# Delta stage's end of a two-layer trunk kernel: output tile 0 read back in the last round, last stores awaited one stage later, last sample states in their own buffer

## What is computed

```
cs = silu(c);  per layer i: mod = cs @ w_ada[i] + b_ada[i]  -> shift, scale, gate for mixer and for MoE
h = x * (1 + scale_m) + shift_m
y = retention(h)            for layer 0   (4 heads, dk 256, dv 512)
y = gated_delta_net(h)      for layer 1   (16 value heads of 128 x 128, causal conv of width 4)
x = layer_norm(ALPHA * x + (1 + gate_m) * y)
h = x * (1 + scale_f) + shift_f
y = moe(h)                  16 experts in 4 groups, top 2, one shared router
x = layer_norm(ALPHA * x + (1 + gate_f) * y)
outputs: y_prompt, y_sample, and the new recurrent states of both mixers and of the convolution
```

## Time and profile before

| | us |
|---|---|
| three timed runs | 2217.83 median, 2215.38 to 2229.18 |
| the profiled execution | 2212.75 |
| its span, first to last instruction | 2210.9 |
| PE busy in the span | 1863.6 (84%) |
| granted TensorE clock, mean over the span | 0.908 of full speed |
| delta's first projection to the first product of mixer_end for layer 1 | 1024.4 to 1806.7 |
| DMA traffic | 397.20 MB, mean 180 GB/s |
| of it in the two queues named "instruction" | 2.28 MB |

### The profile page before, as it was taken

The page is one execution under the profiler, slowest core; times in us unless marked ns, Lnnn a source line. Parts: engine busy times, 40 slices in busy tenths (PEclk is TensorE's granted clock), DMA queues, the critical chain, the costliest instruction groups (busy, mean ns, idle before and its releaser), DMA issues. The chain is left out here.

```text
span 2210.9 us, 35700 instructions
## 1 busy us (share of the span) xinstructions
PE 1863.6 (84%) x15037; PEld 971.6 (44%) x15037; DVE 795.4 (36%) x1646; ACT 378.8 (17%) x835; POOL 355.6 (16%) x456
## 2 busy tenths in 40 slices
PE   5999999999899859956989989988987769949970
PEld 3443443433334432324566656755754634433320
DVE  0123323223322330015665465555535323240008
ACT  1010000100000011114332242232232100001111
POOL 0010110101102200022521122032031002120114
PEclk8999999999989979977989989989998779959985
DMA  9364638457170199978321033034035574078964
GB/s 341 123 226 174 255 121 295 164 177 255 68 248 38 43 379 398 398 276 270 129 93 46 15 116 110 12 106 121 8 108 159 177 217 137 27 270 298 403 241 147
DMA packets 234652, 397.20 MB, mean 180 GB/s; under 512 B 17597, under 2 KB 90949, under 8 KB 234438
## 3 DMA queue, kind: packets, MB, share of 16 engines
q1 hardware_dynamic: 228542, 373.43, 48.1%
q0 software_dynamic: 5952, 21.50, 2.6%
HBM read 301.38 MB, written 93.51 MB: 179 GB/s over the span
## 5 line engine op out<-in xcount | busy, mean ns | idle before, releaser
L562 PE MATMUL bank<-ring,hT 128*128 128x512 f32 x768 | 346.5, 602 | 3.3 <-PEq L277 2.2
L562 PEld LDWEIGHTS bank<-ring,hT 128*128 128x128 f32 x768 | 142.8, 191 | 189.2 <-issue 186.5
L1194 PE MATMUL bank<-hT,ring 128*128 128x272 f32 x768 | 220.3, 422 | 0.0
L2344 PE MATMUL bank<-expert_w,exp_xT 128*32 128x512 f32 x1152 | 177.9, 625 | 14.4 <-DMA expert_w<-in_moe_w_gu_dram 10.4
L3020 PE MATMUL bank<-ring,oT 128*128 128x512 f32 x384 | 174.7, 617 | 13.3 <-DMA oT<-oT_spill 12.7
L1194 PEld LDWEIGHTS bank<-hT,ring 128*128 128x128 f32 x768 | 142.8, 199 | 35.0 <-issue 9.5
L1188 PE MATMUL bank<-ring,hT 128*128 128x512 f32 x256 | 125.0, 617 | 0.0
L3020 PEld LDWEIGHTS bank<-ring,oT 128*128 128x128 f32 x384 | 75.4, 198 | 108.0 <-issue 94.9
L2344 PEld LDWEIGHTS bank<-expert_w,exp_xT 128*32 128x32 f32 x1152 | 47.5, 115 | 125.6 <-issue 120.4
L2368 PE MATMUL bank<-expert_w,exp_aT 128*32 128x512 f32 x576 | 88.7, 606 | 10.6 <-DMA expert_w<-in_moe_w_down_dram 9.2
L1864 DVE SCALAR_TENSOR_TENSOR dn_y<-dn_pre,dn_conv,dn_y 128x568 f32<-128x568 f32 x96 | 89.3, 930 | 3.4
(11 more groups left out here) (478 smaller groups left out, 2559.8 us busy)
## 6 DMA issues: line engine op xcount, KB each, us to landing
ring<-in_w_ada_dram SPq DMA_DIRECT2D x24, 2048.0 KB, 9.2
expert_w<-in_moe_w_gu_dram SPq DMA_DIRECT2D x24, 2048.0 KB, 15.8
expert_outputs<-ret_zeros SPq DMA_DIRECT2D x15, 2048.0 KB, 10.4
expert_w<-in_moe_w_down_dram SPq DMA_DIRECT2D x24, 1024.0 KB, 16.3
ring<-in_ret_w_in_dram SPq DMA_DIRECT2D x8, 2048.0 KB, 13.9
ret_Ss<-in_state_ret_dram SPq DMA_DIRECT2D x32, 512.0 KB, 5.5
out_dram<-ret_Ss SPq DMA_DIRECT2D x32, 512.0 KB, 3.9
oT<-in_moe_w_gu_dram SPq DMA_DIRECT2D x8, 2048.0 KB, 21.0
```

What stands on the lines that cost most here:

```text
L562: last = pe.matmul(ps[u % 2][:, :], core.hT[:, k, tok(t)], core.ring[:, w % RING, k, :], start=(k == 0), stop=(k == KD - 1))
L1194: mm = pe.matmul(ps[U % 2][:, 0:HALF], core.ring[:, w % RING, k, c * P:(c + 1) * P], core.hT[:, k, half * HALF:(half + 1) * HALF], start=( ...
L2344: last = pe.matmul(ps[v][G * j:G * (j + 1), :], xT[:, v, k, G * j:G * (j + 1)], wgu[of[j] % SLOTS][:, k, :], start=(k == 0), stop=(k == KD ...
```

## The change

- `state_in`: state 7 (the last, `n == 2 * G - 1`) goes to `SLAST`, laid over the first half of `qr`, whose last user is round 2. It is loaded without a wait in SP's step C3 of the last chunk of round 2, behind the store of `S`. The loads of states 1 to 6 are as they were. PE's S1 waits for both of the last two loads from state 6 on.
- `va` and `qr` become pairs of buffers; the first of `va` is `core.reuse`, which outlives the stage. In C5 of x = 13 SP waits for store 12 and reads tile 0 of oT_spill (1 MB) into it (`first_tile`, semaphore `first_in`).
- `modulations_out` moves from behind the schedule to C5 of x = 15, ahead of the wait for the last tile.
- The last store of `oTr` and the last store of `S` count on `late_out`, a semaphore that belongs to no stage; delta's end no longer waits for them. mixer_end waits for it in front of its reads of tiles 2 to 4.
- In mixer_end SP issues extra, tile 1, x, gates, vectors, then that wait, then tiles 2 to 4. Tile 0 is used from `core.reuse`; `core.oT` has 128 columns fewer, and the expert slot in it moves with its end.
- `dn_norm_g` is loaded earlier, on the semaphore `gate_in` (96 instead of 80), and `ins` is gone. `S` and `oTr` are allocated later.

```diff
@@ class Core
+        self.first_in, self.late_out = (ctx.enter_context(nc.semaphore(n)) for n in ("first_in", "late_out"))
...
+    def first_tile(self):
+
+        return self.reuse[:].rearrange("p c n -> p (c n)")[:, 0:16 * P].rearrange("p (k n) -> p k n", n=P)
@@ delta
-        va, qr = st.sb("va", [P, 2, 4, NTOK]), st.sb("qr", [P, 2, 4, NTOK])
+        va, qr = ([a, st.sb(n, [P, 4, NTOK])] for n, a in (("va", core.reuse), ("qr", st.sb("qr0", [P, 4, NTOK]))))
...
+        first_tile = core.first_tile()
+        SLAST = qr[0][:].rearrange("p c n -> p (c n)")[:, 0:2 * DECB * P].rearrange("p (k b v) -> p k b v", k=2, v=P)
+        states = lambda n: SLAST if n == 2 * G - 1 else SS
...
+                sp.dma_start(ng[:], d["dn_norm_g"].broadcast_to([P, P])).then_inc(s["gate_in"], 16)
                 core.load(sp, core.mix[1][0] + RING - 1)
...
-                sp.dma_start(ng[:], d["dn_norm_g"].broadcast_to([P, P])).then_inc(s["ins"], 16)
...
                 def state_in(n):
                     for k in range(2):
-                        if n:
+                        if 0 < n < 2 * G - 1:
                             sp.wait_ge(s[f"ss_out{k}"], 16 * n)
-                        sp.dma_start(SS[:, k], d["state_dn"][0, :, 2 * n + k].rearrange("b p v -> p b v")
+                        sp.dma_start(states(n)[:, k], d["state_dn"][0, :, 2 * n + k].rearrange("b p v -> p b v")
                                      ).then_inc(s[f"ss_in{k}"], 16)
...
                     if what == "C5":
+                        if x == NC * G - 1:
+                            core.modulations_out(sp, 16, 8, res)
+                        if x == NC * (G - 1) + 1:
+                            sp.wait_ge(s["oT_out"], 16 * x)
+                            sp.dma_start(first_tile, oTd[:, :, tok(0)]).then_inc(core.first_in, 16)
                         sp.wait_ge(s["oT_kept"], x + 1)
-                        sp.dma_start(oTd[:, 4 * g:4 * g + 4, tok(i)], oTr[:]).then_inc(s["oT_out"], 16)
+                        sp.dma_start(oTd[:, 4 * g:4 * g + 4, tok(i)], oTr[:]).then_inc(
+                            core.late_out if x == NC * G - 1 else s["oT_out"], 16)
                     if what == "C3" and i == NC - 1:
                         sp.wait_ge(s["S_done"], 4 * (x + 1))
-                        sp.dma_start(d["dn_p"][0, 0, 4 * g:4 * g + 4].rearrange("h p v -> p h v"), S[:]).then_inc(s["S_out"], 16)
+                        sp.dma_start(d["dn_p"][0, 0, 4 * g:4 * g + 4].rearrange("h p v -> p h v"), S[:]).then_inc(
+                            core.late_out if g == G - 1 else s["S_out"], 16)
+                    if what == "C3" and x == NC * (G - 1) - 1:
+                        state_in(2 * G - 1)
...
-                        if n + 1 < 2 * G:
+                        if n + 1 < 2 * G - 1:
                             state_in(n + 1)
...
-                core.modulations_out(sp, 16, 8, res)
                 sp.wait_ge(core.ada_out, core.OUT["delta"])
...
-                sp.wait_ge(s["oT_out"], 16 * NC * G)
+                sp.wait_ge(s["oT_out"], 16 * (NC * G - 1))
                 sp.wait_ge(s["oTs_out"], 16 * G)
-                sp.wait_ge(s["S_out"], 16 * G)
+                sp.wait_ge(s["S_out"], 16 * (G - 1))
...
-                            pe.wait_ge(s[f"ss_in{k}"], 16 * (n + 1))
+                            pe.wait_ge(s[f"ss_in{k}"], 16 * (n + 1 if n < 2 * G - 2 else 2 * G))
...
-                pool.wait_ge(s["ins"], 16)
+                pool.wait_ge(s["gate_in"], 96)
@@ mixer_end
-                for t in range(NT):
-                    if l:
-                        sp.dma_start(oT[:, :, tok(t)], d["oT"][:, :, tok(t)]).then_inc(oT_in[t], 16)
-                    if t == 0:
-                        sp.dma_start(extra[:], core.out_block(l, 3)).then_inc(s["extra_in"], 16)
+                sp.dma_start(extra[:], core.out_block(l, 3)).then_inc(s["extra_in"], 16)
+                if l:
+                    values_in(sp, 1)
                 r.load(sp, x_from)
                 r.gates(sp)
                 r.vectors(sp)
+                if l:
+                    sp.wait_ge(core.late_out, 32)
+                    for t in range(2, NT):
+                        values_in(sp, t)
...
                     if l:
-                        pe.wait_ge(oT_in[t], 16)
+                        pe.wait_ge(oT_in[t] if t else core.first_in, 16)
@@ build
+        core.reuse = core.sb(ctx, "reuse", [P, 4, NTOK])
...
-            core.oT = core.sb(mid, "oT2", [P, 16, NTOK])
+            core.oT = core.sb(mid, "oT2", [P, 16, NTOK - P])
```

## The result

In ten runs each, before and after by turns on one chip, the medians are 2211.99 us before (2197.59 to 2229.18) and 2201.82 after (2187.02 to 2207.99). The ratio is 0.9942, with a 95% interval of 0.9917 to 0.9967: about 12.8 us less, and between 7.3 and 18.4. (The ratio is not the quotient of the two medians, which lie 10.2 us apart.) The forecast was 2201.5, a change within 1%.

What follows compares the result with a forecast made beforehand. PE, busy 84% of the span, was taken to bound the kernel, so gains are the holes closed in its work. State 8.0 plus seam 8.3 make 16.3 us, from 2217.83 to 2201.5, range 2191 to 2213.

Steps and rivals of the forecast that it cites:

- The total: Whole kernel: 16.3 us gained, from a timed median of 2217.83 to 2201.5 us.
- The seam: Between delta and the next stage: earlier stage end plus PE starting without waiting for the tile, 8.3 us together.
- mod_rows: End of delta: its stores issued earlier let the stage end at 1796.7 instead of 1798.9, 2.2 us sooner.
- the tile: Start of the next stage: PE's first wait is for a tile already landed, 6.1 us gained.
- The cover of the tile's read: Last round: some 8 us before PE needs ACT's copy hide the read's delay of tile 13's store; cost 0, bound 1.
- What follows: Next stage: tile 0's rows turned at 1856.1, later transfers in time; no term, up to 6 us lost if vectors come late.
- The state part: State 7's own buffer at L1429: the 6.80 us hole goes whole, plus most of 1.69 from the clock; 8.0 taken.
- rival A: State 7's hole is replaced by a longer PE wait for DVE at L1450; gain 10, 2207.8 us; 12 in 100.
- one such stop in 210 us: PE's stops for issue from 1670 to 1880 us: one of 4.8 us counted, as evidence against the slower case.
- Rival D: Slower than before: moved transfers meet PE's instruction loads, 4.8 us a stop, five stops make 2225.5; 4 in 100.
- a stop beside a ring load: PE's instruction fetch beside bulk transfers: by the skill's packet-by-packet turns a stop would cost near 0, against a 4.8 us row.
- Rival C: PE's clock stays up from 1700 to 1710 and in a later stretch; gain 22.7, 2195.1 us; 10 in 100.

Runs made afterwards that it cites:

- e7_tile_late: Kernel after the change, with tile 0 read back as the next stage's first DMA instead of in the last round; executed once, only its trace read.
- e10_again: The kernel after the change, unchanged, timed again beside the kernel with three further edits: 2199.93 us, ratio to before 0.9942.
- e3_ring_late: Kernel after the change, with the ring load behind the bias rows held until PE has ended state 7's products; executed once, only its trace read.
- e5_mod_early: Kernel after the change, with the mod_rows stores issued ahead of the stage's last ring load; executed once, only its trace read.
- e1_state_only: Kernel before the change, with only state 7's own buffer and early load added: 2203.73 us, ratio to before 0.9958.
- e8_p2_late: Kernel after the change, with the fourth modulation block's ring load held until PE is past its old issue stop; executed once, only its trace read.
- e6_mod_end: Kernel after the change, with the mod_rows stores put back at the stage's end; executed once, only its trace read.

## Why the prediction was right, and where it was not

**The total** was right: 2201.5 forecast, 2201.82 measured. That it is right to 0.3 us is luck. The gain forecast was 16.3 us; the ratio gives 12.8 with 16.3 inside its interval, the traces give 11.8 and the medians 10.2. The medians of before differ from one set of runs to another, 2217.83 where I started and 2211.99 in the comparison, and these 5.8 us made up for the gain that was missing.

**The seam** was right in its mechanism and, within the scatter of D3, in size. Forecast 8.3, measured 8.5: mod_rows 2.2 against 2.3, the tile 6.1 against 6.0. That the parts fit to 0.1 us is luck again, since by the other traces mod_rows is worth 1.0 to 2.4. PE's first product was released by the queue and not by a DMA, as said, at 4.17 us. The forecast let mod_rows be awaited behind the dn_S store and the ring load, and SP did wait 1.3 us for them. The store of dn_S took 7.9 us and the tiles' stores 2.6, as before. The cover of the tile's read was needed and held: ACT waited 3.5 us for the store of tile 13, which it does not do in e7_tile_late, and PE had no use for its copy until 1794.31. What follows was in time: PE turned tile 0's rows at 1856.40 without a wait (forecast 1856.1), and DVE's vectors were there after 28.5 us (forecast near 33).

**The state part** was mis-sized: forecast 8.0, measured 3.4 (3.9 in e10_again). The step that failed is the one that took the 6.80 us whole, "since no row shows anything else late". The wait at L1466 stayed at 4.53, so rival A is false. What was late next were PE's instructions for the end of these products. No row that I had read shows them, because the hole itself covered them, but the trace of before does: the packet moves at 1682.76, when PE had been ready since 1681.68. With 1.73 us for 55 products from there, and 2.6 us from a packet to PE's next product, the stop to expect was about 2 us even with the packet at its old time, an estimate from these traces; the ring load did the rest. I had also counted "one such stop in 210 us", where that trace has four, of 4.75, 1.57, 1.31 and 0.73 us. By terms: the hole gone, 6.8 less; the 64 products in 2.53 us instead of 3.64, 1.1 less; the new stop, 4.3 more; the short stop ahead of it, at L204, 0.3 more (1.04 against 0.73); together 3.3, beside the 3.4 of D1. Rival D named this mechanism and was given 4 in 100, as five stops that turn the result. It came once, and the forecast's sum had no term for that. With the ring load held back D1 is 7.3 less than before, near the 8.0.

**The packets.** The Trainium skill ("DMA: Bandwidth & Descriptors", Queues, rings and completion order) has a DMA engine take turns between its queues packet by packet. By that the prediction worked out a stop beside a ring load of near 0, and already had the row of 4.8 us against it. These runs bear out the row: the same packet came 4.47 us after the stop ahead of it with the ring load in the engines and 1.14 us without. The same page and section of the Trainium skill has the write that raises a semaphore land only behind all earlier writes of its DMA engine. The trace of the kernel after agrees, with 7.9 us for the store of dn_S behind the ring load against 2.6 for the tiles' stores.

**The clock.** Rival C wanted the clock to stay up from 1700 to 1710. It did not: the grant is 0.50 from 1705 to 1710 after the change, and 0.50 from 1690 to 1700 in e3_ring_late, where the same wait of 4.53 us ends at 1691.27. The new stop costs clock as well. These windows of the kernel after (us, busy us by engine with instructions, PEclk, DMA share, GB/s) show the stop, and the fall with it:

```profile
1683.00:1688.00 5.00, 3.96 (x137) 3.06 (x140) 2.15 (x4) 0.00 (x0) 0.73 (x1) 1.00 0.93 239
1688.00:1693.00 5.00, 0.72 (x21) 0.46 (x16) 0.00 (x0) 0.00 (x0) 0.00 (x0) 0.76 0.84 307
```

PE is busy 0.72 us of the second five and the grant goes from 1.00 to 0.76 on average. In e3_ring_late, where PE stands still for only 0.99 us there, it is at the full 2.4 GHz, 1.00, in both windows:

```profile
1675.00:1680.00 5.00, 4.27 (x147) 3.22 (x140) 2.27 (x5) 0.00 (x0) 1.00 (x1) 1.00 0.56 145
1680.00:1685.00 5.00, 3.68 (x137) 2.44 (x126) 1.67 (x4) 2.43 (x8) 0.66 (x3) 1.00 0.43 125
```

That is the second part of the stop's price, and a small one within D1: of the 3.9 us by which D1 fell in e3_ring_late, 3.3 are the stop, 0.3 the last nine products (0.49 us instead of 0.80) and 0.3 the stop at L204 (0.73 instead of 1.04).

## What to carry to other kernels

A hole in the timeline hides everything that arrives during it, instruction loads among them; before its whole length is booked as gain, ask what else is fetched in it, and look at the instruction queue's packets. Where a stop for "issue" stands beside a bulk load, hold that load back for the few microseconds: two such waits and one store moved ahead of a load gave nearly as much again as the whole change (11.5 us of medians against 12.8). And a store that a barrier waits for belongs ahead of the last big load on its queue.

## What the runs showed of the hardware that was not expected

A 16 KB packet of PE's instructions came 3.3 us later beside a 2 MB load than in nearly empty engines, and PE's next product followed such a packet by 2.3 to 2.6 us at every stop that I followed. PE's stops for issue end, in all twelve traces, at places 256 records apart or a multiple of it, the share of one packet. With nearly empty engines about 1 us of the stop is left (0.99, 0.98). The size of one stop is not fixed by its place: at the 56th product of state 7 it was 4.28 in two profiled executions of the kernel after and in e5_mod_early, 4.00 in e1_state_only, e7_tile_late and e8_p2_late, and 2.90 in e6_mod_end, with the same code there.
